# Last two weight pieces of an output projection multiplied tile by tile, with the first LayerNorm woven between them (one Trainium2 core)

## The reference, cut to what matters

```
mixed = concat(attention, conv) @ w_out            # 2048 x 2048        <--
h = layer_norm(2 ** 0.25 * h + mixed, ln1_g, ln1_b)                     <--
q = h @ peer_wq                                    # 2048 x 2048, then sub-key scores, top-16 of two halves
experts, gates = top-16 of the 256 candidates per head (8 heads)
y = sum over 128 experts of gate * gelu(u[expert] . h) * v[expert]
h = layer_norm(2 ** 0.25 * h + y, ln2_g, ln2_b)
out = h + sigmoid(h @ ple_gate) * (p @ ple_proj)
new_k, new_v = the old caches, shifted by the new rows   # 128 copies of 1 MB from memory to memory
```

## Time and profile before

| what | us |
|---|---|
| median of 3 runs | 2494.15 (2490.1 to 2497.6) |
| profiled execution, span of the trace | 2482.5 |
| PE busy in it | 1882.2 (76%) |
| DVE busy | 1716.9 (69%) |
| POOL busy | 1114.4 (45%) |
| ACT busy | 926.8 (37%) |

### The profile page before, as it was taken

One profiled execution on the slowest core, in us unless ns is written; L12 is line 12 of the kernel. 1 busy time (PEld: TensorE's weight loads), 2 busy tenths in 40 slices (PEclk: granted clock), 3 DMA queues, 4 the chain that ended last, 5 costly groups with the idle time before them and its releaser, 6 DMA issues.

```text
span 2482.5 us, 27095 instructions
## 1 busy us (share of the span) xinstructions
PE 1882.2 (76%) x10342; PEld 1559.1 (63%) x10342; DVE 1716.9 (69%) x2410; ACT 926.8 (37%) x1461; POOL 1114.4 (45%) x484
## 2 busy tenths in 40 slices
PE   6998899899959945444230323899999999999798
PEld 5885778787859734434120223777777777787676
DVE  1066232422146998987999999899898998897723
ACT  3223122223223311111470894644445444444332
POOL 3663233335626446887767884122222222220154
PEclk9998899999989977676555556999999999999899
DMA  9997999997999889999999997499999999998547
GB/s 346 390 387 271 370 414 415 384 382 268 372 345 358 319 329 373 407 421 422 421 391 393 422 421 296 183 396 382 375 389 361 357 373 372 361 383 301 211 186 262
DMA packets 131568, 882.00 MB, mean 355 GB/s; under 512 B 18962, under 2 KB 20562, under 8 KB 55540
## 3 DMA queue, kind: packets, MB, share of 16 engines
q1 hardware_dynamic: 76148, 477.65, 50.4%
q0 software_dynamic: 55296, 402.68, 40.2%
HBM read 871.28 MB, written 141.63 MB: 408 GB/s over the span
## 4 chain that ended last, share of the span: by engine, by line
issue 29%; PE 23%; DVE 21%; POOL 14%; DMA 11%; ACT 2%; POOLq 0%; SPq 0%; ACTq 0%; DVEq 0%
DVE expert_rows L1311 7%; PE psum L1506 7%; PE psum L1508 7%; DMA v_raw<-in_peer_v 7%; PE psum L1507 7%; POOL expert_rows L577 6%; POOL w_lo L547 6%; DMA expert_rows<-in_peer_u,experts 4%; DVE v_lo L1448 2%; DVE x_tokens L1392 2%; DVE expert_rows L1383 2%; ACT v_hi L876 1%; PE psum L1785 1%; DVE chunk_one_hot L1252 1%; DVE chunk_one_hot L1254 1%
## 5 line engine op out<-in xcount | busy, mean ns | idle before, releaser
L547 POOL TENSOR_TENSOR w_lo<-w_raw,w_hi 128x2048 fp32r<-128x2048 f32 x80 | 372.8, 4660 | 463.4 <-ACT w_hi L608 463.4
L1311 DVE SCALAR_TENSOR_TENSOR expert_rows<-expert_rows,x_tokens 128x2048 f32<-128x2048 f32 x238 | 538.5, 2289 | 49.3 <-DMA expert_rows<-in_peer_u,experts 48.3
L577 POOL DMA_INDIRECT expert_rows<-in_peer_u,experts x238 | 462.1, 1942 | 173.0 <-DVE expert_rows L1311 103.6
L1506 PE MATMUL psum<-v_hi,gate_matrix_hi 128*128 128x512 f32 x1024 | 406.5, 397 | 29.6 <-DVE v_lo L1448 29.0
L876 ACT ACTIVATE v_hi<-v_raw 128x1024 fp32r<-128x1024 f32 x256 | 271.5, 1061 | 396.9 <-DMA v_raw<-in_peer_v 314.3
L1507 PE MATMUL psum<-v_lo,gate_matrix_hi 128*128 128x512 f32 x1024 | 400.2, 391 | 0.0
L1508 PE MATMUL psum<-v_hi,gate_matrix_lo 128*128 128x512 f32 x1024 | 400.1, 391 | 0.0
L1448 DVE TENSOR_TENSOR v_lo<-v_raw,v_hi 128x1024 fp32r<-128x1024 f32 x256 | 309.7, 1219 | 74.4 <-ACT v_hi L876 73.9
L608 ACT ACTIVATE w_hi<-w_raw 128x2048 fp32r<-128x2048 f32 x80 | 153.2, 1915 | 375.0 <-PE psum L1508 278.2
L1506 PEld LDWEIGHTS psum<-v_hi,gate_matrix_hi 128*128 128x128 f32 x1024 | 192.8, 188 | 94.2 <-issue 32.7
L1785 PE MATMUL psum<-one_hot_first_gated,one_hot_second 128*128 128x128 f32 x320 | 74.7, 409 | 214.4 <-ACT one_hot_first_gated L791 210.3
(11 more groups left out here) (329 smaller groups left out, 3372.5 us busy)
## 6 DMA issues: line engine op xcount, KB each, us to landing
v_raw<-in_peer_v SPq DMA_DIRECT2D x256, 512.0 KB, 7.1
out<-in_state_attn_k SPq DMA_DIRECT2D x64, 1020.0 KB, 10.7
out<-in_state_attn_v SPq DMA_DIRECT2D x64, 1020.0 KB, 10.9
w_raw<-in_w_in SPq DMA_DIRECT2D x48, 1024.0 KB, 8.1
cache_part<-in_k_parts SPq DMA_DIRECT2D x40, 1024.0 KB, 10.9
cache_part<-in_v_parts SPq DMA_DIRECT2D x40, 1024.0 KB, 12.5
w_raw<-in_w_out SPq DMA_DIRECT2D x16, 1024.0 KB, 7.0
w_raw<-in_peer_wq SPq DMA_DIRECT2D x16, 1024.0 KB, 7.5
```

The costliest lines, as they stand in the source:

```text
L547: nc.gpsimd.tensor_tensor(l_, r_, h_.bitcast(f32), ALU.subtract).then_inc(w_lo_ready, 1)
L577: pool.indirect_dma_start(ring[slot_of(n)][:, :], None, u_tab, bass.IndirectOffsetOnAxis(idx_p[:, t - 1, j:j + 1], 0)).then_inc(u_in[slot_ ...
L1311: V.scalar_tensor_tensor(out=g, in0=g, scalar=1.0, in1=xt[:, t, :], op0=ALU.mult, op1=ALU.mult, accum_out=hdot[:, t, j:j + 1]).then_inc(u_ ...
L1506: MM(out, lh, rh, start=start, stop=False)
```

## The change

Pieces 60 and 61 (the first two of the last chunk) are multiplied as before. Pieces 62 and 63 are multiplied together, tile by tile: both pieces for tile 0, then both for tile 1, then both for tile 2. A new semaphore `out_tile_mm` tells DVE when tile 0 and tile 1 are complete. On DVE the residual and the moments of the last 512 columns are no longer done for three tiles at once but per tile, in front of that tile's norm (`last_sums`). `w_used` for the two pieces is still raised with tile 2. Tile 1 is transposed into the banks of tile 0 (`T_MID`), since banks 4 to 6 are still being summed. The second group of low parts moves behind the last norm. On SP the two loads for the norm move ahead of piece 60, and four of the twelve cache copies behind pieces 64 and 65 move to a place ahead of the third load of `peer_v`, with a wait for the 235th prompt row.

```diff
-T_MID = [(t, g, g + (4 if t else 0)) for t in range(3) for g in range(4)]
+T_MID = [(t, g, g + (4 if t == 2 else 0)) for t in range(3) for g in range(4)]
@@ SP
             for c in range(1, 4):
+                if c == 3:
+                    sp.dma_start(ln1[:, 0, :], ...).then_inc(ln1_in, 16)
+                    sp.dma_start(ln1[:, 1, :], ...).then_inc(ln1_in, 16)
                 load_chunk(w_out, c, 48 + c * PPC, 0, (2, 1, 2, 1))
-            sp.dma_start(ln1[:, 0, :], ...).then_inc(ln1_in, 16)
-            sp.dma_start(ln1[:, 1, :], ...).then_inc(ln1_in, 16)
             for k in range(2):
                 load_piece(wq, k, 64 + k, k)
-            copies(12)
+            copies(8)
...
                 if m == 2:
+                    sp.wait_ge(u_free, len(VEC_ROWS) - 3)
+                    copies(4)
                     sp.wait_ge(x_acc, 2)
@@ ACT
             layer_norm_root(0)
             layer_norm_root(1)
-            transposed_hi(1, 0, 8)
+            transposed_hi(1, 0, 4)
             layer_norm_root(2)
-            transposed_hi(1, 8, 12)
+            transposed_hi(1, 4, 12)
@@ DVE
-            for c in range(4):
+            for c in range(3):
...
+            def last_sums(t):
+                r, cc = TILES[t][1], slice(3 * CW, 4 * CW)
+                if t < 2:
+                    dve.wait_ge(out_tile_mm, t + 1)
+                else:
+                    dve.wait_ge(w_used, 64)
+                o = xt[0:r, t, cc]
+                m = V.scalar_tensor_tensor(out=o, in0=o, scalar=ALPHA, in1=PS[0:r, 4 + t, :], op0=ALU.mult, op1=ALU.add)
+                if t == 2:
+                    m.then_inc(acc_free, 1)
+                    dve.wait_ge(acc_free, 16)
+                else:
+                    link(m)
+                if t == 0:
+                    link(V.tensor_tensor(xt[0:TS, 0, cc], xt[0:TS, 0, cc], PS[TS:128, 4, :], ALU.add))
+                link(V.bn_stats(bst[0:r, t, 3, :], xt[0:r, t, cc]))
...
             dve.wait_ge(ln1_in, 32)
+            last_sums(0)
             layer_norm(0, 0, ln1, False)
+            last_sums(1)
             layer_norm(1, 1, ln1, False)
-            transposed_lo(1, 0, 8)
+            transposed_lo(1, 0, 4)
+            last_sums(2)
             layer_norm(2, 2, ln1, False)
-            transposed_lo(1, 8, 12)
+            transposed_lo(1, 4, 12)
@@ PE
             for h in range(2):
                 pe.wait_ge(acc_free, 13 + h)
-                for k in range(PPC):
+                for k in range(PPC if h == 0 else 2):
                     token_piece(56 + h * 4 + k, k, 4 * h)
+            for t in range(3):
+                for k in (2, 3):
+                    m = token_piece(60 + k, k, 4, tiles=(t,))
+                if t < 2:
+                    m.then_inc(out_tile_mm, 1)
```

More of the change, by code:

```diff
@@ L275, in decoder_step @@
         att_ok, att_hi, att_lo, conv_lo = sem("attention_done"), sem("attention_hi"), sem("attention_lo"), sem("conv_lo_ready")
+        out_tile_mm = sem("out_tile_in_psum")
         var_ok, std_ok = sem("ln_var_ready"), sem("ln_std_ready")
@@ L484, in _ @@
             for c in range(1, 4):
+                if c == 3:
+                    sp.dma_start(ln1[:, 0, :], ln1_g.rearrange("a d -> (a d)").partition_broadcast(128)).then_inc(ln1_in, 16)
+                    sp.dma_start(ln1[:, 1, :], ln1_b.rearrange("a d -> (a d)").partition_broadcast(128)).then_inc(ln1_in, 16)
                 load_chunk(w_out, c, 48 + c * PPC, 0, (2, 1, 2, 1))
-            sp.dma_start(ln1[:, 0, :], ln1_g.rearrange("a d -> (a d)").partition_broadcast(128)).then_inc(ln1_in, 16)
-            sp.dma_start(ln1[:, 1, :], ln1_b.rearrange("a d -> (a d)").partition_broadcast(128)).then_inc(ln1_in, 16)
             for k in range(2):
                 load_piece(wq, k, 64 + k, k)
-            copies(12)
+            copies(8)
             for c in range(4):
@@ L1527, in token_piece @@
                     m.then_inc(w_used, 1)
+                return m
             def feature_piece(pc, k, bank):
```

## The result

The changed kernel takes 2510.3 us (median; 2509.5 to 2512.1) against 2494.2: 16.1 us more. The ratio on record is 1.0077 with a 95% interval of 1.0057 to 1.0097; it is not the quotient of the two medians, which is 1.0065. In microseconds the recorded ratio is 19, its interval 14 to 24. The forecast was 2504.5 with a range up to 2509. The direction held; by the medians the size was 1.6 times the forecast, and the time is 1.3 us outside the range. That is beyond the 0.3% that a measurement here can tell from no change.

The account below looks back on a forecast made before the run. The stretch from the end of piece 63 to the first `peer_wq` matmul was taken to lie on the path. Terms 4.75 + 0.5 + 4.0 + 1.2 = +10.45 us on 2494.15 gave 2504.6, forecast 2504.5, range 2495.5 to 2509.

Parts of the forecast that it names:

- (A): Main case: gate, DVE chain, norm's loads and late copies simply add up, +10.45 us; chance 0.58.
- gate at piece 63, clock steady: End of `w_out` on PE: 56 instead of 32 matmuls remain once piece 63's low part is ready; +4.75 us.
- clock behind that wait: PE matmuls after a wait run partly at 1.2 GHz: 1.6 us lost per wait, counted only in (D).
- (D): Rival: more than the sum, PE's clock drops behind both waits and copies reach their upper bound; +15 us, 2509; chance 0.11.
- norm's loads, wait: PE waits for piece 60, delayed behind the norm's 2 MB in the queue; +4.0 us, bounds 0 to 4.4.
- DVE chain, E to `peer_wq`: From the last `w_out` matmul's end to the first `peer_wq` matmul, early sums win nothing; +0.5 us, bounds -1 to +2.
- four copies fewer in the full queue: Behind pieces 64 and 65, 4 MB less buys nothing since PE has no gap; 0, at most 10.4 us.
- four copies behind row 235: Copies share DMA with the last prompt rows and delay row 238; +1.2 us, bounds 0 to 2.5.
- the relief of 0.7: Piece 63 no longer waits for its transfer behind the norm's loads; -0.7 us off the gate's cost.
- the lockout on POOL: POOL's two subtractions hold up DVE's first norm; alternatively DVE slips between them, its second pass waits, and the end is the same.
- (B): Rival: the queue's slack swallows the norm's loads; +6.4 us, 2500.6, within no change; chance 0.24.
- (C): Rival: not slower, four copies fewer shorten the start of `peer_wq` and the row phase by 10.4 us; 2494; chance 0.07.

Follow-up runs that it names:

- filled_wait: Changed kernel with 18 unread matmuls into bank 7 between pieces 62 and 63 of tile 0, filling PE's wait; ratio 1.0065 against the unchanged kernel.
- only_tiles: Changed kernel with the norm's two loads and the four cache copies put back in their old places; ratio 1.0050 against the unchanged kernel.
- only_norm_loads: Unchanged kernel with only the norm's two loads moved ahead of piece 60; ratio 1.0024.
- only_copies: Unchanged kernel with only four of the twelve cache copies moved behind row 235; ratio 1.0020.
- roots_first: Changed kernel with ACT's three roots and the copies of tiles 0 and 1 ahead of rounding pieces 64 and 65; ratio 1.0004 against the unchanged kernel.
- aa_before: Unchanged kernel profiled a second time, no edit; ratio 0.9984, span 2491.4 us.
- best_8_late: Changed kernel with tile order for piece 63 alone, ACT's roots first, old transfers except eight copies behind row 238; 2483.6 us, 0.9962 against the unchanged kernel.

## Why the prediction was wrong

**The mechanism of (A) was right, two of its sizes were not.** Term by term, forecast against stages and traces:

| term | forecast | shown |
|---|---|---|
| gate at piece 63, clock steady | +4.75 | +4.6 (wait of 4.82 us where before had 0.19) |
| clock behind that wait | 0 in (A), 1.6 in (D) | +2.4 (15.1 for 12.7 us; 2.2 given back by filled_wait) |
| norm's loads, wait | +4.0 | +2.7 to 3.2 |
| clock behind that wait | 0 in (A), 1.6 in (D) | +1.6 (8 matmuls at 0.43) |
| DVE chain, E to `peer_wq` | +0.5 | +1 (33.6 for 32.5 to 32.9; 34.1 in the first trace) |
| four copies fewer in the full queue | 0 | 0 |
| four copies behind row 235 | +1.2 | +5.4 to +6.7 |
| sum | +10.45 | 18 to 19; 16.1 by the medians, 14 to 24 by the interval |

In only_tiles, where the norm's loads still follow piece 63, the wait at the gate is 5.55 us, 5.4 more than before; with the loads moved it is 4.6 more. That bears out both the 5.45 of the 24 matmuls and the relief of 0.7 that the forecast took off.

**The step that failed is the price of the copies.** I let the copies take half of the engines for the last megabyte, took 1.2 us and put the upper bound at 2.5; the runs show 5.4 to 6.7. Between the use of rows 237 and 238, 43 full packets of the copies passed and 35 of the gathers: near half by number, ten to one by bytes, because a packet of the copies is 64 KB and one of the gathers 8 KB. The Trainium skill's rule (DMA: Bandwidth & Descriptors, Queues, rings and completion order) that an engine goes round its queues packet by packet agrees with these counts, if what the profile counts as a packet is what that page calls one, which no run here shows. My turning it into half of the bandwidth was the error. The bound was no bound. I had also read the wrong stretch: the 72 GB/s of the earlier trace rows are those of 1530 to 1583, and the copies go out at 1521.7, where the rows still come at 422 GB/s with a DMA share of 1.01 (windows view of before, 1517:1523).

**The clock stood in the wrong case**, a term of 4.0 us that (A) puts at nothing. I had the row that shows half speed behind a sparse stretch and kept it for (D) at a chance of 0.11. In every trace whose PE waited 2.47 to 5.55 us among the `w_out` matmuls the matmuls behind ran at half speed; here it is part of the price of the wait. (A) and (D) were one case, and with the clock in it the forecast would have been 14.5. That (D)'s sum, +15, comes near the measured 16.1 is in part luck: its copies were too cheap by 3 to 4 us and its loads too dear by about 1.

One more slip, which does not touch the forecast itself: the bounds given for the terms of (A) add to +3.7 at least and +14.4 at most, not to the +6.7 and +13 that its chances were worked out from.

**What held.** The direction; the wait of DVE for the root (12.16 us, forecast some 10); the lockout on POOL, in the form that I gave as the alternative, with the same end; 56 matmuls behind the gate; piece 60 released by DMA and landing in 11.0 us, between the bounds; (B) and (C) refuted by only_norm_loads and only_copies. The aside in (C), that a free root would win 1 us at best, was wrong: 16 us (roots_first). It kept a lockout in place that depends on the very order that would be changed.

## What to carry to other kernels

An order by tiles over two weight pieces puts the later piece's gate in front of most of the work; over the last piece alone it cost nothing here. Before an overlap is built, follow the small helper on the other engine: here one root stood behind a rounding that waited for the very matmuls to be overlapped, and moving it was worth more than all the rest. Count a wait of 2.5 us or more inside dense matmuls at its length plus about 2 us of half clock, and do not let large-packet copies start while a small-packet gather is still needed: wait for the last row, not for the third last. And take a second trace of the unchanged kernel before the difference of two spans is shared out among the stages: here one execution began two stages at half clock and the other did not.

## What the runs showed of the hardware that was not expected

- The granted clock fell to the 1.2 GHz level behind waits of PE of 2.47 to 5.55 us among dense matmuls; the 512-column matmuls then stood 0.43 us apart for 3.4 us (8 of them) behind 2.66 us, and for 4.5 us (10) behind 4.82 (changed kernel). Behind waits of 0.83 us (filled_wait) and 1.76 us (roots_first, PEclk 1.00 in 665.6:668) it did not fall.
- Executions of the same code began `w_out` and `peer_wq` at either level of the clock: 3.1 and 2.0 us lost in aa_before, 0.6 and none in before.
- Two queues with different packet sizes: 43 packets of 65,280 B (2.81 MB) against 35 of 8 KB (0.29 MB) in 8.4 us (changed kernel, 1539.9:1548.3).
- DVE and POOL hold each other up by about the length of a whole instruction, in both directions. With both operands in SBUF a DVE pass of 2.35 us took 6.46 and ended 2.14 us behind POOL, as the held pass of before did, and POOL's pair took 11.07 instead of 8.99 in the same stretch; in best_8_late 0.69 us on DVE became 5.06 beside a subtraction of 4.64. DVE's sums from PSUM, 1.88 us for three, were not held.
